# Output projection with a PSUM bank pair per head group, token factors applied on the way out, and the loop's guests moved

## The reference, cut to what matters

```python
def merge_groups(o_fox, o_nsa, g_fox, g_nsa, w_out):
    of = rmsnorm(o_fox.reshape(B, T, W_FOX), g_fox)
    on = rmsnorm(o_nsa.reshape(B, T, W_NSA), g_nsa)
    return jnp.concatenate([of, on], axis=-1) @ w_out
```

## Time and profile before

| | us |
|---|---|
| median of 3 runs | 1231.75 |
| their range | 1228.39 to 1233.62 |
| the profiled execution, as timed | 1230.65 |
| its span, first to last instruction | 1228.8 |
| PE busy in the span | 1169.5 |
| DVE, ACT, POOL busy | 528.4, 419.2, 153.8 |
| mean granted TensorE clock, of full speed | 0.979 |

### The profile page before, as it was taken

The page is one execution under the profiler, slowest core; times in us unless marked ns, Lnnn a source line. Parts: engine busy times, 40 slices in busy tenths (PEclk is TensorE's granted clock), DMA queues, the critical chain, the costliest instruction groups (busy, mean ns, idle before and its releaser), DMA issues.

```text
span 1228.8 us, 23220 instructions
## 1 busy us (share of the span) xinstructions
PE 1169.5 (95%) x9460; PEld 1080.0 (88%) x9466; DVE 528.4 (43%) x757; ACT 419.2 (34%) x731; POOL 153.8 (13%) x154
## 2 busy tenths in 40 slices
PE   8999999999999899998988888989999999999994
PEld 6999999999999799995455555979999999999994
DVE  4433432333433753454265666454433333433334
ACT  6222221222233542225233465453222211222342
POOL 0111100011111000222113033210011000011110
PEclk9999999999999999999988998999999999999997
DMA  6322223222223133315562211121222223232221
GB/s 274 103 74 97 87 78 111 103 75 96 78 87 111 54 121 116 109 53 148 140 169 89 105 69 36 69 69 64 74 102 92 68 90 125 74 103 90 65 86 70
DMA packets 49008, 117.53 MB, mean 96 GB/s; under 512 B 8186, under 2 KB 24954, under 8 KB 43138
## 3 DMA queue, kind: packets, MB, share of 16 engines
q1 hardware_dynamic: 45746, 110.55, 27.4%
q10 hardware_dynamic: 3184, 5.88, 1.3%
HBM read 107.79 MB, written 7.97 MB: 94 GB/s over the span
## 4 chain that ended last, share of the span: by engine, by line
PE 86%; DVE 6%; issue 2%; SPq 2%; ACT 2%; DMA 1%; POOL 0%; DVEq 0%; ACTq 0%; POOLq 0%
PE ps L1483 75%; PE ps L1492 2%; PE ps L1673 1%; PE ps L1643 1%; PE ps L1610 1%; PE ps L1627 1%; DVE UT L995 1%; SPq L555 1%; DVE H L999 1%; DVE row_max L1153 1%; DVE PTS L480 1%; DMA X<-X 1%; PE ps L1884 1%; DVE XL L975 1%; PE ps L1576 0%
## 5 line engine op out<-in xcount | busy, mean ns | idle before, releaser
L1483 PE MATMUL ps<-XH,WH 128*128 128x260 f32 x1872 | 383.4, 286 | 8.4 <-DVE XL L975 8.0
L1483 PE MATMUL ps<-XH,WL 128*128 128x260 f32 x1872 | 377.6, 283 | 0.0
L1483 PE MATMUL ps<-XL,WH 128*128 128x260 f32 x1872 | 377.0, 283 | 0.0
L411 ACT CAST WH<-RAW 128x1024 fp32r<-128x1024 f32 (+2 forms) x183 | 175.0, 956 | 525.6 <-PE ps L1483 521.4
L1483 PEld LDWEIGHTS ps<-XH,WH 128*128 128x128 f32 x1872 | 290.7, 189 | 13.1 <-DVE XL L975 8.3
L1483 PEld LDWEIGHTS ps<-XH,WL 128*128 128x128 f32 x1872 | 289.0, 189 | 0.0
L1483 PEld LDWEIGHTS ps<-XL,WH 128*128 128x128 f32 x1872 | 288.3, 189 | 0.0
L414 DVE TENSOR_TENSOR WL<-RAW,WH 128x1024 fp32r<-128x1024 f32 (+2 forms) x183 | 204.8, 1119 | 158.1 <-ACT WH L411 156.8
L1483 PE MATMUL ps<-UL,WH 128*128 128x260 f32 x704 | 141.9, 283 | 0.0
L1483 PE MATMUL ps<-UH,WL 128*128 128x260 f32 x704 | 141.5, 282 | 0.0
L1483 PE MATMUL ps<-UH,WH 128*128 128x260 f32 x704 | 141.4, 282 | 0.0
(11 more groups left out here) (248 smaller groups left out, 956.1 us busy)
## 6 DMA issues: line engine op xcount, KB each, us to landing
RAW<-in_w_gu SPq DMA_DIRECT2D x44, 1024.0 KB, 4.8
RAW<-in_w_down SPq DMA_DIRECT2D x16, 768.0 KB, 4.5
RAW<-in_w_in SPq DMA_DIRECT2D x11, 1024.0 KB, 4.8
RAW<-in_w_down SPq DMA_DIRECT2D x16, 640.0 KB, 4.2
KF<-in_fox_k SPq DMA_DIRECT2D x16, 256.0 KB, 4.1
VF<-in_fox_v SPq DMA_DIRECT2D x16, 256.0 KB, 4.1
RAW<-in_w_out SPq DMA_DIRECT2D x4, 1024.0 KB, 5.0
H<-in_x SPq DMA_DIRECT2D x4, 520.0 KB, 7.0
```

The lines of the kernel that those rows point to most:

```text
L411: nc.scalar.copy(WH[:, par, 0:width], RAW[:, slot, j, 0:width]).then_inc(w_hi, 1)
L1483: q = nc.tensor.matmul(ps[:, 2 * slot + half, 0:HALF], w[:, par, cols], x[:, kt0 + kt, half * HALF:(half + 1) * HALF], start=first and kt ...
```

## The change

- The product of each group of heads (contraction tiles 0 to 3 and 4 to 7) is summed in a pair of banks of its own (slots 2(t % 2) and 2(t % 2)+1; eight banks for two output tiles in flight). `XH` and `XL` are made from `OT` without the token factor. When a tile is taken out, DVE multiplies each of the two sums by its group's factor and adds them: three operations and one temporary, `OU`.
- So the multiplications of `OT` by `OR` go (four on POOL, four on DVE), and with them the wait for the factors before `XH`. Guest 40 goes; both groups' sums over the partitions are done in the middle of output tile 0, the logarithms beside it. The sample tokens' squares are made apart, by three small DVE operations after `AT_DECODED` (`o_new`), and the loop's squares cover 512 columns.
- The remaining ten guests move: 14, 17..20 become 15, 17, 20, 23 (pick before the compressed keys), 25 to 26, 27 to 30, 29 to 32, 32 to 35, 35 to 37. The copy of the new window key goes from one step ahead of its guest to two. The compressed values of tile 4 are multiplied at the end of step 33 instead of in step 27's `weigh`.
- Squares, `XH`, `XL`, splits and POOL's sums go to steps given by four tables.
- At the projection's end PE waits for the last tile to be out (`ydone_b`, 8) ahead of `output_squares`, which reuses its banks.

```diff
-AT_HIDDEN, AT_CMP_KV, AT_CMP_SCORES, AT_CMP_BACK = 14, 18, 20, 27
-AT_PICK, AT_FOX_KEYS, AT_NSA_KEYS, AT_TURN, AT_VALUES, AT_DECODED, AT_SUMS = 19, 22, 25, 29, 32, 35, 40
+AT_HIDDEN, AT_CMP_KV, AT_CMP_SCORES, AT_CMP_BACK = 15, 20, 23, 30
+AT_PICK, AT_FOX_KEYS, AT_NSA_KEYS, AT_TURN, AT_VALUES, AT_DECODED = 17, 22, 26, 32, 35, 37
+CMP_LATE = 33
+OUT_SQUARES = (28, 29, 31, 32, 36, 40, 47)
+OUT_HIGH = (38, 39, 41, 42, 44, 45, 48)
+OUT_SPLIT = (43, 49)
+OUT_LOW = (41, 42, 44, 45, 48, 49, 50)
...
 # ACT, in the loop
+                if m in OUT_SQUARES:
+                    output_square(OUT_SQUARES.index(m), SEQ)
...
+                if m in OUT_HIGH:
+                    output_high(OUT_HIGH.index(m))
+                if m in OUT_SPLIT:
+                    split(IT_OUT + OUT_SPLIT.index(m))
...
-                    if tiles and m >= pairs_until(tiles[0]) + 4:
+                    if tiles and m >= pairs_until(tiles[0]) + 4 and (tiles[0] != 4 or m >= CMP_LATE):
                         pair_out(tiles.pop(0))
...
 # ACT, after the loop
-            act.wait_ge(sem("att_out"), 8)
-            output_square(7)
-            output_log(1)
-            output_rstd(1)
-            for t in range(4, 8):
-                output_high(t)
+            output_high(7)
+            output_square(7, TOK)
+            for g in (0, 1):
+                output_log(g)
+            for g in (0, 1):
+                output_rstd(g)
...
 # DVE, in the loop
-                if m == AT_NSA_KEYS - 1:
+                if m == AT_NSA_KEYS - 2:
...
+                if m == AT_DECODED + 1:
+                    new = HID[:, 0, 0:8 * DEC].rearrange("p (t b) -> p t b", b=DEC)
+                    dve.wait_ge(sem("o_all"), 1)
+                    link(nc.vector.tensor_tensor(new, OT[:, :, SEQ:TOK], OT[:, :, SEQ:TOK], ALU.mult))
+                    for g in (0, 1):
+                        nc.vector.reduce_sum(OACC[:, g, SEQ:TOK], view(HID[:, 0, :], 4 * DEC * g, [[1, DEC], [DEC, 4 - g]]),
+                                             AX.X).then_inc(sem("o_new"), 1)
+                if m in OUT_LOW:
+                    low("o", "out", OUT_LOW.index(m))
+                if m == OUT_SPLIT[0] + 3:
+                    split(IT_OUT)
...
 # DVE, after the loop
+            low("o", "out", 7)
+            split(IT_OUT + 1)
+
+
+            dve.wait_ge(sem("orstd"), 2)
             for t in range(KT):
                 dve.wait_ge(used, IT_OUT + t + 1)
-                nc.vector.tensor_copy(two(Y[:, t, :]), halves(t % 2)).then_inc(sem("ydone_b"), 1)
+                nc.vector.tensor_tensor(two(Y[:, t, :]), halves(2 * (t % 2)), two(OR[:, 0, :]), ALU.mult)
+                link(nc.vector.tensor_tensor(two(OU[:, t % 2, :]), halves(2 * (t % 2) + 1), two(OR[:, 1, :]), ALU.mult))
+                nc.vector.tensor_tensor(Y[:, t, :], Y[:, t, :], OU[:, t % 2, :], ALU.add).then_inc(sem("ydone_b"), 1)
                 split(IT_OUT + t + 2)
...
 # POOL, in the loop
-                elif m == AT_DECODED + 2:
-                    output_sum(1)
-                    output_sum(2)
-                    output_sum(3)
-                elif m == AT_SUMS:
-                    output_sum(5)
-                elif AT_SUMS + 1 <= m < AT_SUMS + 5:
-                    t = m - AT_SUMS - 1
-                    pool.wait_ge(sem("orstd"), 1)
-                    nc.gpsimd.tensor_tensor(OT[:, t, :], OT[:, t, :], OR[:, 0, :], ALU.mult).then_inc(
-                        sem("onormed"), 1)
+                for t in (1, 2, 3, 5):
+                    if m == OUT_SQUARES[t]:
+                        output_sum(t)
...
 # PE
+                    if m == CMP_LATE:
+                        compressed_values(4)
...
+            def by_groups(t):
+
+                for g in (0, 1):
+                    if t == 1:
+                        pe.wait_ge(sem("oss_ln"), g + 1)
+                    slot = 2 * (t % 2) + g
+                    for kt in range(4 * g, 4 * g + 4):
+                        if t == 0:
+                            pe.wait_ge(sem("xlo"), since("xlo", "o", kt + 1))
+                        cols = slice(kt * P, kt * P + P)
+                        for p, (w, x) in enumerate(((WH, XH), (WH, XL), (WL, XH))):
+                            for half in (0, 1):
+                                q = nc.tensor.matmul(ps[:, 2 * slot + half, 0:HALF], w[:, (IT_OUT + t) % 2, cols],
+                                                     x[:, kt, half * HALF:(half + 1) * HALF],
+                                                     start=kt % 4 == 0 and p == 0, stop=kt % 4 == 3 and p == 2)
+                    if t == 0 and g == 0:
+                        pe.wait_ge(sem("oacc"), 3)
+                        pe.wait_ge(sem("o_new"), 2)
+                        all_partitions(OACC[:, 0, :], 2).then_inc(sem("oss"), 1)
+                        pe.wait_ge(sem("att_out"), 8)
+                        pe.wait_ge(sem("oacc"), 5)
+                        all_partitions(OACC[:, 1, :], 3, stop=False)
+                        pe.wait_ge(sem("osq"), 8)
+                        all_partitions(OSQ[:, 2, :], 3, start=False).then_inc(sem("oss"), 1)
+                q.then_inc(used, 1)
+
+            for t in range(KT):
                 ready(IT_OUT + t)
                 if t >= 2:
                     pe.wait_ge(sem("ydone_b"), t - 1)
-                products((IT_OUT + t) % 2, KT, XH, XL, t % 2)
+                by_groups(t)
+            pe.wait_ge(sem("ydone_b"), KT)
             output_squares("b")
```

More of the change, by code:

```diff
@@ L344, in layer_kernel @@
         OACC = on.put("OACC", [P, 2, TOK], F32)
+        OU = at("OU", [P, 2, TOK], pa0)
         osq = Region(f0 + 8192, 3 * tile_b)
@@ L823, in decode_exp, with output_square @@
                                      accum_out=dsum[:, n:n + 1]).then_inc(sem("d_exp"), 1)
-            def output_square(t):
-                dst = OACC[:, t // 4, :] if t % 4 == 0 else OSQ[:, t % 4 - 1, :]
-                nc.scalar.activation(dst, OT[:, t, :], ACT.Square).then_inc(sem("osq"), 1)
+            def output_square(t, width):
+                act.wait_ge(sem("att_out"), t + 1)
+                if t == 5:
+                    act.wait_ge(sem("oacc"), 3)
+                dst = OACC[:, t // 4, 0:width] if t % 4 == 0 else OSQ[:, t % 4 - 1, 0:width]
+                nc.scalar.activation(dst, OT[:, t, 0:width], ACT.Square).then_inc(sem("osq"), 1)
             def output_log(g):
                 act.wait_ge(sem("oss"), g + 1)
-                nc.scalar.activation(two(OR[:, g, :]), halves(2), ACT.Ln, scale=1.0 / 512,
+                nc.scalar.activation(two(OR[:, g, :]), halves(2 + g), ACT.Ln, scale=1.0 / 512,
                                      bias=const("eps")[:, 0:1]).then_inc(sem("oss_ln"), 1)
@@ L1312, in follow @@
                                          AX.X).then_inc(sem("d_o"), 1)
-                if m in (AT_SUMS + 2, AT_SUMS + 3):
-                    split(IT_OUT + m - AT_SUMS - 2)
-                if AT_SUMS + 5 <= m < AT_SUMS + 9:
-                    low("o", "out", m - AT_SUMS - 5)
+                if m == AT_DECODED + 1:
+                    new = HID[:, 0, 0:8 * DEC].rearrange("p (t b) -> p t b", b=DEC)
[8 more added lines that the diff above has]
+                    split(IT_OUT)
             def attention():
@@ L1444, in output_sum @@
                     pool.wait_ge(sem("oacc"), n - 1)
-                nc.gpsimd.tensor_tensor(OACC[:, g, :], OACC[:, g, :], OSQ[:, t % 4 - 1, :], ALU.add).then_inc(
+                nc.gpsimd.tensor_tensor(OACC[:, g, 0:SEQ], OACC[:, g, 0:SEQ], OSQ[:, t % 4 - 1, 0:SEQ], ALU.add).then_inc(
                     sem("oacc"), 1)
@@ L1812, in guest @@
                     decoded()
-                elif m == AT_SUMS:
-                    pe.wait_ge(sem("oacc"), 3)
-                    all_partitions(OACC[:, 0, :], 2).then_inc(sem("oss"), 1)
             def emptied(m):
@@ L1874, in _ @@
             attention()
-            def operand(t, kt):
-                if t == 0:
-                    pe.wait_ge(sem("xlo"), since("xlo", "o", kt + 1))
-                cols = slice(kt * P, kt * P + P)
-                for p, (w, x) in enumerate(((WH, XH), (WH, XL), (WL, XH))):
-                    for half in (0, 1):
-                        q = nc.tensor.matmul(ps[:, 2 * t + half, 0:HALF], w[:, (IT_OUT + t) % 2, cols],
-                                             x[:, kt, half * HALF:(half + 1) * HALF],
-                                             start=kt == 0 and p == 0, stop=kt == KT - 1 and p == 2)
-                return q
@@ L1903, in _ @@
-            operand(0, 7).then_inc(used, 1)
-            operand(1, 5)
-            operand(1, 6)
-            operand(1, 7).then_inc(used, 1)
-            for t in range(2, KT):
+            def by_groups(t):
[22 more added lines that the diff above has]
+                q.then_inc(used, 1)
```

69 lines of the change are left out of this document (12 added, 57 removed).

## The result

The changed kernel takes 1222.44 us (median of 8 runs, 1218.42 to 1225.41); the kernel before, on the same chip, 1228.85 (8 runs, 1225.92 to 1233.62). The ratio is 0.9943, 95% interval [0.9921, 0.9964], 6.4 us faster. The profiled execution took 1222.94 us with a span of 1221.1 and a granted clock of 0.978, so against the profiled execution of before it is 7.7 us shorter in either measure. The sum had 11.9.

A forecast was written before the change was run, and what follows sets the result against it. TensorE was taken as the bound, losing time only where it idles or runs slowly. 14.2 us gained in the loop, 0 in the projection and 2.3 lost at its end gave 11.9 saved: 1220 us predicted, range 1213 to 1226.

The forecast's parts named there:

- Guest 40 and the multiplications: Step 40 to the projection: removing the guest gains 4.9 us, removing POOL's and DVE's multiplications of OT gains 2.5.
- the hidden windows: Guest 14 to 15: one more step of attention is done before their DMA lands, gaining 2.0 us (1 to 2.0).
- the compressed keys: Compressed keys, scores and pick moved within steps 17 to 23: activation ends earlier for its reader, gaining 2.0 us (-2 to 6).
- Window keys: Guest 25 to 26, key column copied earlier: the 2.3 us wait and a half-clock stretch go, gaining 3.0 us (0 to 4).
- tile 4's values: Tile 4's compressed values at step 33 instead of 27: the 1.1 us wait for PCT goes, gaining 1.0 us.
- turning: Turn 29 to 32, values 32 to 35, decoded 35 to 37: more time for decode weights, gaining 0.8 us (0 to 1.6).
- squares: Squares from step 28 on, with POOL adds in steps 29, 31, 32, 40 meeting DVE's scalings, cost 2.0 us (0 to 3.5).
- My own test: Mechanism counts as wrong if the loop from the hidden windows' end on is less than 6 us shorter.
- rival C: Most of the loop's half clock goes, gaining half of 15 us on top of the sum: about 1212 us; chance 0.11.
- The end: Projection's end: nothing hides the last tile's three DVE operations, PE idles 2.1 us; cost 2.3 us (1.2 to 3.5).
- Rival A: Attention loop: late DVE copies replace each removed single wait, leaving some 4.6 us gained, about 1227 us; chance 0.21.
- Rival B: The full-clock stretch 681.10 to 724.26 gets gaps and a lower clock: about 1240 us, slower; chance 0.08.

The follow-up runs named there:

- run 9: Kernel before with only the new window key's copy one step earlier, two steps ahead of its guest; 1224.62 us, ratio 0.9969.
- the changed kernel again: The changed kernel, unaltered, run and profiled a second time as a yardstick; 1223.76 us, ratio 0.9952 to the kernel before.
- run 6: Changed kernel with DVE's first multiplication of the last output tile done while PE still sums the second group; 1218.85 us, again 1221.61.
- run 1: Changed kernel with its ten guests, tile 4's compressed values and the window key's copy back at their old places; 1215.92 us, again 1218.50.
- run 8: Changed kernel, guests at old steps, last tile's first multiplication during PE's second-group sum, window key's copy two steps ahead of its guest; 1213.93 us.
- run 4: Changed kernel with six guest constants altered, the compressed scores at step 21 instead of 23; 1216.96 us, ratio 0.9908 to the kernel before.
- run 3: Kernel before with POOL's four multiplications of OT left out, each replaced by a small write; 1226.01 us, ratio 0.9968.
- run 7: Changed kernel with guests at their old steps and the last tile's first multiplication done during PE's second-group sum; 1219.11 us, ratio 0.9918.
- run 2: Kernel before with only the ten guests moved to their new steps and the sums' guest at 41; 1226.73 us, ratio 0.9987.
- run 5: Changed kernel with compressed scores at step 21 and the last tile's first multiplication during PE's second-group sum; 1214.70 us, ratio 0.9875.

## Why the prediction was right and where it was wrong

*Guest 40 and the multiplications: right, low.* 7.4 predicted, 8.65 in this execution; in all but one of the other executions with deferred factors the stretch is 28.0 us, 11.1 shorter, with a clock of 1.00. The missing part is half clock: the term counted what was idle and only part of what was slow. The granted clock after 740 was to be above 0.9: it is 0.76 here and 1.00 there. The split takes 1.21 us, as forecast. DVE's cycle of 8 to 9 us came and hurt nothing: steps 40 to 43 hold 9.29 us of DVE work in 10.36 us, and PE idles 0.4.

*Guests up to step 25: near in size, in part by luck.* From step 13 to 25, with the same guests done, the changed kernel is 4.5 us shorter against 4.0 predicted: 3.3 by step 16 for the hidden windows (2.0), 1.2 after it for the compressed keys (2.0). The first part holds: all four profiles of this order take 26.2 us from step 13 to 16, where the kernel before took 29.5 (28.0 in run 9). The second does not: from step 16 to 25 the changed kernel again and both executions of run 6 take 43.1 to 43.4 us, against 42.6 before. The gain of 2.0 for the compressed keys is thus not shown.

*Guests from step 25 on: wrong, and this is the step that failed.* Window keys 3.0, tile 4's values 1.0, turning 0.8 and squares -2.0 were to gain 2.8 us; the stretch is 4.3 longer, and 3.2 in the changed kernel again. The squares' term was near beside the moves (1.2 to 2.3) and doesn't show in run 1. The window-key term was right by itself (runs 8 and 9), and still shows in PE's waits. What the sum lacked is in the part on the compressed keys, "scores 20 to 23": it followed the PE guest and the DVE work with it, and of POOL only the key columns. Three POOL operations on `SCM` follow that guest by fixed steps, 6.2 us, with three memsets of 1.6 queued behind the first; they were moved next to DVE's scalings with it. The prediction had the price of such a meeting in the earlier trace rows, about 1.1 us for each POOL operation of 1.3, and used it for the squares and the multiplications, not for these. Run 4, which moves them away, is 3.4 to 4.5 us shorter in this stretch. My own test, the loop from the hidden windows' end on at least 6 us shorter, doesn't settle it: from step 16 on it is 142.8 us before and 137.2 after, 5.5 shorter, but 6.3 to 7.1 shorter in the changed kernel again and in run 6. The shape is plain all the same: by step 40 nothing of the forecast gain is there, and the part from step 16 to 40 is 3.1 to 4.9 us longer in all four. The 7 us between step 36 and the projection are 4.8 here and 7.0 to 7.2 in those three, though one guest, 37, now lies inside; that cut was badly chosen.

*The idle and the clock.* PE's idle from step 13 to 40 fell by 3.8 us (18.5 to 14.65; 15.55 in the changed kernel again), while its busy time rose by 3.65 for one record more. "Half of the 15 us" for rival C and "a gap is paid twice over 2 us" both took the clock as following single gaps. Run 9 shows a gap paid twice. But gaps of over 2 us aren't always: the one of 2.37 us before the compressed keys left the clock full in run 1 again and in run 8, and it fell there in the kernel before and in runs 3, 7 and 9. At the projection's end the same gap of 2.13 us left the clock full in two executions of the changed kernel, while it fell in run 4 and in both executions of run 1, here the second:

```profile
797.23 1.51 PE L1481 MATMUL ps<-ACC,consts 128*128 128x260 f32 x4 [2.13 <-DVE Y L1349]
798.54 1.94 PE L1481 MATMUL ps<-SQ,consts 128*128 128x260 f32 x4
```

*The end: right within its range, for a reason that varies.* 1.3 us here, 2.6 in run 1 again; 2.3 was predicted with bounds of 1.2 and 3.5. The last multiplication to the end of the last sum of squares takes 4.15 us, inside the 4 to 6 named. I had written that I would be wrong here if the clock stayed full; in the changed kernel it did, so the fall of the clock was no part of its cost. The Trainium skill ("TensorE: Matmul & The Clock Gate", "Why this matters for your kernels"), by which this gap leaves the clock alone, fits these two executions and not the other three, one of which is shown above.

*The projection* cost nothing, as predicted: three operations and a split fit in a tile's 5.8 us. *Rival A* (late copies take every wait's place) did not happen by its own row: it fell from 10.5 to 7.0 us in 11 waits instead of 14. Part of it came about at other lines: the single waits removed before step 40 were 7.8 us in the earlier trace rows, and PE's idle there fell by 3.8 (2.9 in the changed kernel again). *Rival B's* lower clock came about in part in steps 25 to 40, 0.97 to 0.87 here and to 0.95 and 0.92 in other executions, and run 2 has 0.92 without added squares. The stretch lost 3 to 4 us and not 11, and the one after 40 outweighed it.

The forecast was thus near by luck: a gain that was put too low (after 40) stood against one that did not come (steps 25 to 40).

## What to carry to other kernels

When a step of a hand-ordered loop moves, list what every engine issues at a fixed distance behind it, GpSimd's work first, and look what each piece will lie beside on VectorE: here a guest's constant moved 8 us of GpSimd work next to VectorE's scalings and turned an expected gain of 3 us into a loss of 3 to 4. Undo the parts of a bundled change one at a time even when it is faster as a whole: the fastest kernel here by its median keeps the deferral and one of the moves, with an early end, and gains 15.6 us where the bundle gains 6.4. And where identical code scatters by several us in one stretch, compare the stretches that don't, before the whole.

## What the runs showed of the hardware

- *A DVE scaling, split or `XL` that meets a POOL operation ends only after it.* The scalings at 674.51 end at 677.38, 0.6 us after the POOL operation that began at 674.42 ended (676.77); alone they take 0.87. The first of the two ends 0.22 us after it. The XL of the earlier trace rows at 756.26 ends at 758.07, 0.56 after the POOL add of the earlier trace rows. The POOL operation on `SCM` takes 1.91 or 1.92 us in all three kernels, so the delay is all DVE's. Not every DVE operation pays: in run 4 a copy out of PSUM and the row maxima beside the POOL operation of 667.05 keep their times (0.69 us at 667.46). The price of a meeting is thus what is left of the POOL operation when DVE comes, up to 2.3 us here, and not a fixed 1.1. The Trainium skill says the same ("SBUF — State Buffer", "Who interferes with whom": one pair of ports, an exclusive lock, the later one blocks until the first is done), and this trace agrees. The memsets count too: at 658.77 the first POOL operation has 1.2 us left, but the first scaling takes 2.89 us and ends at 661.66, 0.28 after the last of the three memsets, and the pair is 2.34 late. In run 6 again it got in ahead of the third memset, which then took 0.80 us instead of 0.52: there POOL was held up too.
- *Half clock without an idle gap.* In run 8 the clock is low in one stretch only between step 13 and the projection:

```profile
638.00:642.60 4.60, 4.60 (x72) 3.94 (x70) 3.16 (x7) 0.81 (x4) 0.00 (x0) 1.00 1.01 308
642.60:649.60 7.00, 6.60 (x38) 3.74 (x40) 4.85 (x14) 2.25 (x7) 2.01 (x3) 0.51 0.69 195
```

  Before the clock fell PE was busy all of the 4.60 us, mostly with the compressed scores, 64 records of 32 columns each that began at 637.68 behind a gap of 0.40. In 13 of the 14 profiled executions the clock falls while these 64 records run or at most 1.2 us behind them, for 3.4 to 10.2 us (7 here); in run 5 it had fallen 1.0 us ahead of them. The other intervals between step 13 and the projection lie elsewhere from one execution of a kernel to the next, 13.7 us in all in one of run 1 and 23.9 in the other. What decides them stays open.
